# Feed-forward tiles leave their banks by one VectorE instruction that adds high and low part

## The reference, cut to what matters

```python
def conv_ffn(x, w_up, conv_w, conv_b, w_down):          # first block, D_FF = 2816, FFN_CONV = 3
    h = causal_dwconv(x @ w_up, conv_w, conv_b)
    g, u = h[..., :D_FF], h[..., D_FF:]
    return (jax.nn.gelu(g) * u) @ w_down

def sq_relu_mlp(h, w_up, w_down):                       # second block, D_FF_2 = 4096
    u = jnp.matmul(h, w_up)
    return jnp.matmul(jnp.square(jax.nn.relu(u)), w_down)
```

## Time and profile before

| | |
|---|---|
| median of 3 runs | 1063.78 us (1063.66 to 1064.16) |
| profiled execution | 1063.12 us |
| its span, first to last instruction | 1061.4 us |
| TensorE busy | 1049.2 us, 99% |
| VectorE busy | 775.5 us, 73% |
| ScalarE busy | 614.7 us, 58% |
| GpSimd busy | 120.7 us, 11% |
| data moved | 202.19 MB, mean 190 GB/s |
| granted TensorE clock | 0.998 |

### The profile page before, as it was taken

One profiled execution on the slowest core, in us unless ns is written; L12 is line 12 of the kernel. 1 busy time (PEld: TensorE's weight loads), 2 busy tenths in 40 slices (PEclk: granted clock), 3 DMA queues, 4 the chain that ended last, 5 costly groups with the idle time before them and its releaser, 6 DMA issues.

```text
span 1061.4 us, 15269 instructions
## 1 busy us (share of the span) xinstructions
PE 1049.2 (99%) x6158; PEld 920.3 (87%) x6158; DVE 775.5 (73%) x920; ACT 614.7 (58%) x840; POOL 120.7 (11%) x115
## 2 busy tenths in 40 slices
PE   9999999999999999999998999999999999999997
PEld 7989888888989898888888988888899979888886
DVE  6978877667887789767778956556687868655654
ACT  7657665557566677665657535344575656534432
POOL 0000432220000004662110000000000000000000
PEclk9999999999999999999999999999999999999999
DMA  9934885563554446576551674655274425655551
GB/s 332 341 135 164 293 296 195 174 214 134 187 172 158 159 157 232 187 253 219 166 195 41 238 293 163 204 193 181 97 252 146 137 102 196 221 203 194 176 181 40
DMA packets 31573, 202.19 MB, mean 190 GB/s; under 512 B 3688, under 2 KB 3856, under 8 KB 9104
## 3 DMA queue, kind: packets, MB, share of 16 engines
q1 hardware_dynamic: 28464, 189.16, 50.9%
q0 software_dynamic: 3040, 12.07, 3.4%
HBM read 200.15 MB, written 2.63 MB: 191 GB/s over the span
## 4 chain that ended last, share of the span: by engine, by line
PE 91%; DVE 6%; ACT 2%; issue 1%; POOL 0%; DVEq 0%; ACTq 0%; POOLq 0%
PE wk L673 22%; PE wk L705 14%; PE acc L649 10%; PE acc L650 10%; PE acc L651 10%; PE wk L649 5%; PE wk L650 4%; PE wk L651 4%; PE wk L696 3%; PE acc L696 2%; PE wk L774 1%; DVE w_lo L325 1%; PE acc L705 1%; PE acc L870 1%; DVE x L1716 1%
## 5 line engine op out<-in xcount | busy, mean ns | idle before, releaser
L325 DVE TENSOR_TENSOR w_lo<-raw,w_hi 128x2048 fp32r<-128x2048 f32 x161 | 368.9, 2297 | 49.4 <-ACT w_hi L304 44.3
L304 ACT ACTIVATE w_hi<-raw 128x2048 fp32r<-128x2048 f32 x166 | 316.4, 1909 | 14.4 <-DMA raw<-ws 9.9
L673 PE MATMUL wk<-a_hl,w_hi 128*128 128x512 f32 x1024 | 243.6, 390 | 0.0
L673 PEld LDWEIGHTS wk<-a_hl,w_hi 128*128 128x128 f32 x1024 | 190.5, 188 | 38.8
L649 PE MATMUL acc<-w_hi,b_hl 128*128 128x512 f32 x432 | 168.9, 391 | 0.0
L650 PE MATMUL acc<-w_lo,b_hl 128*128 128x512 f32 x432 | 168.6, 390 | 0.0
L651 PE MATMUL acc<-w_hi,b_hl 128*128 128x512 f32 x432 | 168.1, 389 | 0.0
L705 PEld LDWEIGHTS wk<-a_hl,w_lo 128*128 128x128 f32 x1216 | 155.2, 191 | 5.1
L705 PE MATMUL wk<-a_hl,w_lo 128*128 128x256 f32 x1216 | 158.0, 283 | 0.0
L1602 ACT ACTIVATE region<-wk 128x512 f32<-128x512 f32 x30 | 17.9, 596 | 156.2 <-PE wk L705 156.2
L651 PEld LDWEIGHTS acc<-w_hi,b_hl 128*128 128x128 f32 x432 | 81.1, 188 | 17.2
(11 more groups left out here) (269 smaller groups left out, 1557.4 us busy)
## 6 DMA issues: line engine op xcount, KB each, us to landing
raw<-ws SPq DMA_DIRECT2D x172, 1024.0 KB, 4.8
gain<-gains POOLq DMA_DIRECT2D x13, 512.0 KB, 5.5
raw<-ws SPq DMA_DIRECT2D x12, 256.0 KB, 6.7
region<-rows SPq DMA_DIRECT2D x1, 1664.0 KB, 10.5
lines_dram<-line_dram POOLq DMA_DIRECT2D x1, 1536.0 KB, 8.2
bias<-gains POOLq DMA_DIRECT2D x3, 512.0 KB, 5.0
region<-xT SPq DMA_DIRECT2D x4, 256.0 KB, 5.6
x<-x_rows SPq DMA_DIRECT2D x1, 1024.0 KB, 8.8
```

What stands on the lines that cost most here:

```text
L304: act.activation(w_hi[:, u % HIGH, :], raw[:, u % RAW, :], ACT.Copy).then_inc(hi_ready, 1)
L325: dve.tensor_tensor(low_of(u), raw[:, u % RAW, :], w_hi[:, u % HIGH, :].bitcast(F32), ALU.subtract).then_inc(lo_ready, 1)
L673: pe.matmul(banks[:, m, :], wh[:, k, m * P:(m + 1) * P], a_hl[:, k, :, :].rearrange("p e t -> p (e t)"), start=k == 0, stop=False, skip_gr ...
```

## The change

ScalarE's copies of the right halves go, and with them the SBUF buffers `ffn_low` and `mlp_low`, the `low` semaphores and the table `AHEAD`. VectorE takes a sum by one `tensor_reduce` that reads both halves of both banks (128 x 1024 elements in, 128 x 512 out), as soon as TensorE has finished the unit. In step 0 of each gated phase the sum of (1,0) moves ahead of the last low split of that step; before, it stood behind that split, at the start of step 1.

```diff
+        def by_halves(banks):
+            return banks.rearrange("p m (e t) -> p m t e", e=2)
...
-            def ffn_lows(l, base, n, i, a):
-                s = ffn[l]
-                act.wait_ge(unit_done, ffn_units(base, i)[a] + 1)
-                if i:
-                    act.wait_ge(s["padded"], 2 * (i - 1) + a + 1)
-                act.activation(ffn_low[:, a, :, :], ffn_banks(n, i, a)[:, :, T:2 * T], ACT.Copy).then_inc(s["low"], 1)
...
-                if i not in AHEAD:
-                    ffn_lows(l, base, n, i, 0)
                 if i in BOTH:
                     third_taps(0)
-                    ffn_lows(l, base, n, i, 1)
...
-                act.wait_ge(unit_done, u + 1)
-                if i >= 2:
-                    act.wait_ge(s["summed"], i - 1)
-                act.activation(mlp_low[:, i % 2, :, :], mlp_banks(n, i)[:, :, T:2 * T], ACT.Copy).then_inc(s["low"], 1)
...
-                def summed(a):
-                    dve.wait_ge(s["low"], 2 * i + a + 1)
-                    dve.tensor_tensor(hb[:, p + a, :, 2:HW], ffn_banks(n, i, a)[:, :, 0:T], ffn_low[:, a, :, :], ALU.add)\
-                       .then_inc(s["padded"], 1)
+                def summed(a, i=i):
+                    p = 2 * (i % 2)
+                    dve.wait_ge(unit_done, ffn_units(base, i)[a] + 1)
+                    dve.tensor_reduce(hb[:, p + a, :, 2:HW], by_halves(ffn_banks(n, i, a)), AX.X, ALU.add).then_inc(s["padded"], 1)
...
-                summed(0)
+                if i != 1:
+                    summed(0)
...
                 first_taps(1)
                 if i == 0:
+                    summed(0, 1)
                     split_lo(dve, ub + CUT)
...
-                dve.wait_ge(s["low"], i + 1)
-                dve.tensor_tensor(two(ul[:, p, :]), mlp_banks(n, i)[:, :, 0:T], mlp_low[:, i % 2, :, :], ALU.add).then_inc(s["summed"], 1)
+                dve.wait_ge(unit_done, u + 1)
+                dve.tensor_reduce(two(ul[:, p, :]), by_halves(mlp_banks(n, i)), AX.X, ALU.add).then_inc(s["summed"], 1)
```

More of the change, by code:

```diff
@@ L82 @@
 LN_DONE = 11
-AHEAD = (2, 3)
 BOTH = (1, 2)
@@ L207, in build @@
         hf = view(5248, 4, T)
-        ffn_low = view(7936, 2, 2, T)
         ul = view(0, 3, 2 * T)
         rq = view(1536, 3, 2 * T)
-        mlp_low = view(3072, 2, 2, T)
         y_pooled = view(4096, NB, 2 * T).rearrange("p (h f) m -> p h f m", h=2)
@@ L281, in build @@
         ffn = [{n: sem(f"ffn{l}_{n}") for n in
-                ("pad_zero", "low", "padded", "tap2", "taps", "gelu", "gated", "hid_hi", "hid_lo", "last_gated", "last_lo")} for l in range(2)]
+                ("pad_zero", "padded", "tap2", "taps", "gelu", "gated", "hid_hi", "hid_lo", "last_gated", "last_lo")} for l in range(2)]
         mlp = [{n: sem(f"mlp{l}_{n}") for n in
-                ("low", "summed", "square", "hid_hi", "hid_lo")} for l in range(2)]
+                ("summed", "square", "hid_hi", "hid_lo")} for l in range(2)]
         SPARE = {U_DIFF + 15: o_lo_t[:, :, :].rearrange("p k t -> p (k t)"),
@@ L1503, in ffn_step @@
                     split_hi(act, ffn_units(base, i - LAG)[2] + CUT)
-                if i + 1 in AHEAD:
-                    ffn_lows(l, base, n, i + 1, 0)
                 act.wait_ge(s["taps"], 8 * i + 8)
```

## The result

The changed kernel takes 1069.57 us (median of 5 runs, 1068.97 to 1070.06) against 1063.66 us for the kernel before (1063.41 to 1064.16, 5 runs). The ratio is 1.0056, 95% interval 1.0046 to 1.0067. So it is slower by 5.9 us. The forecast had the direction, but a rise of 3.8 us. The stated range ended at 1069.6 us, which is 5.8 us above the 1063.78 us that it was counted from; the time lies at that end, and the rise just beyond it.

What follows compares the result with a forecast made beforehand. TensorE bounds the kernel, so longer sums cost only where its next unit waits for banks: 1.50 + 1.53 + 0.70 + 0.2 - 0.17 = 3.8 us on 1063.78 gives 1067.5 us, range 1065.2 to 1069.6.

Steps and rivals of the forecast that it cites:

- What bounds the kernel: Inner gated steps: TensorE full at 100.00 of 100 us, VectorE 69.81; VectorE matters only where TensorE waits for banks.
- What one sum costs: All 76 sums: a reduce takes 1217 ns and costs VectorE 0.53 us more each, 40 us of work.
- Rival C: Whole kernel: VectorE becomes the bound and all 40 us show, 1104 us; chance 0.01.
- First wait of a gated phase: Unit (1,1) waits for the sum of (0,1) behind two reduces and starts at 100.26, 1.02 us late.
- What the moved sum saves: Unit (2,0) of gated phases: the hold for the sum of (1,0), 0.29 us, goes.
- Second wait of a gated phase: Unit (3,0) waits for the sum of (2,0), five reduces later at 117.52; 1.50 us later in phase 0, 1.53 in phase 1.
- list of signs of being wrong: Changed profile: a longer reduce, unit (1,1) starting at 99.3, or a wait in steps 4 and later.
- The late loads behind the two splits: SyncE's loads in gated phases start 2.2 and 1.6 us later; costed at nothing, at most 2.2 us per phase.
- Rival D: GpSimd's step 1 product costs VectorE 0.5 to 1 us per gated phase, late loads 0.5: 1069.6 us; chance 0.13.
- rival A: Gated phases: chain to (2,0) has 0.5 us of give, only first waits are real: 1066.3 us; chance 0.25.
- Squared phases: First down unit of phase 0 starts 0.70 us late; unit 3 of phase 1 some 0.2 us.
- Gain behind gated phase 1: First turn of pooling comes 0.17 us sooner, since VectorE's splits no longer wait for ScalarE's copies.

Runs made afterwards that it cites:

- the late reduces alone: Kernel before with reduces only from step 4 in gated and step 3 in squared phases, other sums copy and add: 1063.20 us, ratio 0.9997.
- the run with the moved add: Kernel before with reduces from gated step 4 and squared step 3, sum of (1,0) moved as copy and add: 1062.80 us, repeated 1062.89.

## Why the prediction was wrong in size

**What bounds the kernel: right.** TensorE stays full in the later gated steps, with VectorE at 77.13 of 100 us (69.81 before). In the windows view:

```profile
157.00:257.00 100.00, 100.00 (x529) 86.40 (x528) 77.13 (x82) 56.05 (x58) 25.39 (x14) 1.00 0.57 197
```

**What one sum costs: right.** The reduces take 1220 and 1223 ns, forecast 1217:

```profile
L1908 DVE TENSOR_REDUCE region<-wk 128x512 f32<-128x1024 f32 x42 | 51.2, 1220 | 30.4 <-PE wk L706 30.2
L2078 DVE TENSOR_REDUCE region<-wk 128x512 f32<-128x1024 f32 x30 | 36.7, 1223 | 72.4 <-PE wk L706 72.4
```

VectorE has 41.4 us more work in all, forecast 40. Rival C, in which all of this work would be charged, did not come: 29 us of it are shown to be free by the late reduces alone. The Trainium skill, "VectorE: DVE Perf Modes", section "Rules for kernel authors", warns of tensor_reduce on a hot path. VectorE is no hot path in the inner steps, with 77.13 of 100 us busy.

**First wait of a gated phase: right.** Unit (1,1) starts at 100.71, less the 0.38 of the kernel's start 100.33, forecast 100.26. The restart cost is there: the unit lasts 5.67 us, forecast 5.69. The run with reduces in step 0 alone confirms it.

**What the moved sum saves: right in the trace and wrong in the balance.** The hold at (2,0) is gone, as forecast. What the move lets in was not costed. With it the phase is 0.95 us longer than without it.

**Second wait of a gated phase: this is the step that failed.** It said that the chain to the sum of (2,0) grows by five reduces, 2.67 us, and that the rest keeps its length. The forecast end was 117.52; the reduce ends at 117.83 + 1.22 - 0.38 = 118.67:

```profile
117.83 1.22 DVE L1908 TENSOR_REDUCE region<-wk 128x512 f32<-128x1024 f32 x1
```

The chain of before held 0.5 us (a split) and 0.4 us (the taps) of conflict with GpSimd, and the forecast carried these along as if they were part of the instructions. With the moved reduce the taps have their undisturbed 1.78 us, and the conflict at the two splits is 6.50 - 4.48 = 2.0 us. The difference, 1.1 us, is what is missing in the chain, and TensorE gets it whole, since this wait had no slack left: 1.1 us for each phase, 2.2 of the 5.9 us. The term was mis-sized as 1.50 and measured 2.62 and 2.56. Part of it comes out already at (2,1), whose sum stands behind the same two splits: the forecast gave that place no wait. Its list of signs of being wrong had none for this either: the reduce was not longer, (1,1) was not early, and steps 4 and later have no wait.

In the next step the same conflict costs nothing. The product of step 1 also begins beside a reduce and holds up a split by 0.9 us, where the release behind it has slack:

```profile
118.97 3.19 DVE L322 TENSOR_TENSOR w_lo<-raw,w_hi 128x2048 fp32r<-128x2048 f32 x1
```

The late loads behind the two splits were costed at nothing, and that held: the changed kernel's list of waits has no new one on a weight unit but that of the kernel's start.

Rival D named GpSimd's product and a cost of 0.5 to 1 us a phase, and its 1069.6 us is what came. It was placed at step 1 instead of step 0, where the conflict turned out to be free, and held for unlikely, 0.13. That its number fits is in part luck: it was an estimate of 1.0 us a phase for another place. The rows to do better with were in the trace: the split of 2.78 us beside one of 2.28. They were taken in rival A as a possible gain from the conflict going away, when the question was which VectorE instruction the product would now begin beside. The Trainium skill, "GPSIMD Engine Reference", section "Key points", says that GpSimd shares its SBUF interfaces with VectorE, and that VectorE's instructions with two SBUF inputs contend with it. The traces agree: a pair of low splits goes from 4.48 to 6.50 us and the four taps from 1.79 to 2.23 us, while the sums, which read at most one tensor from SBUF, keep their 0.68 and 1.22 us. The runs show which instructions conflict; that the second SBUF input is the reason is the page's statement, and no run here varies it alone.

**Squared phases: right.** Forecast 0.70 and 0.2, measured 0.74 and 0.17. In phase 0 the third sum ends at 607.62 + 1.22 = 608.84 and the first down unit starts 0.09 us behind it, so the sum is what it waited for, though the profile names no releaser:

```profile
607.62 1.22 DVE L2078 TENSOR_REDUCE region<-acc 128x512 f32<-128x1024 f32 x1
```

```profile
608.93 0.47 PE L650 MATMUL acc<-w_hi,b_hl 128*128 128x512 f32 x1 [0.54 <-issue]
```

Unit 3 in phase 1, which stood at 896.06 before:

```profile
902.12 3.94 PE L674 MATMUL wk<-a_hl,w_hi 128*128 128x512 f32 x16
```

**Gain behind gated phase 1: right.** The first turn of pooling stands at 567.15, 5.35 later than before, where the phase ahead of it is 5.52 later: 0.17, as forecast. It answers to the earlier trace rows:

```profile
567.15 1.95 PE L878 MATMUL wk<-region 128*128 128x128 f32 x16
```

Another 0.06 us come behind it in the junction.

**The range** was too narrow upwards by the same term. It took half of rival D in, while the conflict came in both gated phases at once. Its lower end, 1065.2 us, is a rise of 1.4 us, below the 1.8 with which rival A's part begins; that slip had no effect.

## What to carry to other kernels

Where an engine is full, price a longer instruction on a helper by the slack of each release behind it, place by place: here 54 of 76 longer sums were free and 4 of them cost over 2 us. When the order of two instructions is changed, look also at what a third engine will do in the gap: here GpSimd got hold of SBUF where VectorE's instruction read PSUM. A product that begins there holds up whatever two-input instruction comes next. One that becomes ready during a split waits for it, and may then fall beside the harmless sum, if a sum stands behind that split. A stretched duration in the trace of before is not a property of the instruction, and must be worked out again for the new order.

## What the runs showed of the hardware

GpSimd's 128 x 512 product takes 1.28 to 1.31 us when no low split of VectorE runs as it becomes ready. When one runs, the product lasts until 1.14 to 1.17 us behind the end of that split, in all ten kernels: 2.53 us at 102.91 in the kernel before, 2.83 at 103.49 in the run with the moved add, and 3.14 at 115.07 in the kernel before, where the split had just begun. The two do not share in parts: in the rows above the one that comes first keeps its undisturbed length (1.29 us for the product at 104.43, 2.28 us for the split at 103.55 in the run with the sum at its old place), and the other pays. A unit whose first matmul really waited, with no wait behind it, took 5.67 to 5.70 us in every kernel looked at, against 5.56.
